# Values and normaliser of a head in one product over four banks, and the scores behind the second gate tile

## What is computed

```python
d = b[..., :, None] - b[..., None, :] + ic[..., None, :]          # decays, causal
m_t = jnp.maximum(m_inter, d.max(-1))
w_intra = jnp.exp(d - m_t[..., None]) * jnp.einsum('bhtd,bhsd->bhts', qc, kc)
w_inter = jnp.exp(m_inter - m_t)
num = w_inter[..., None] * jnp.einsum('bhtd,bhde->bhte', qc, C) + jnp.einsum('bhts,bhse->bhte', w_intra, vc)
nq = w_inter * jnp.einsum('bhtd,bhd->bht', qc, n) + w_intra.sum(-1)
h = num / jnp.maximum(jnp.abs(nq), jnp.exp(-m_t))[..., None]
C_new = decay[..., None, None] * C + jnp.einsum('bhs,bhsd,bhse->bhde', w_state, kc, vc)
n_new = decay[..., None] * n + jnp.einsum('bhs,bhsd->bhd', w_state, kc)
# then: hn = rmsnorm over the 256 values of a head; y = (hn * sigmoid(o)) @ w_out
```

## Time and profile before

| | us |
|---|---|
| runs of the kernel | 1204.06, 1206.19, 5891.28 (median 1206.19) |
| the profiled execution, its own time | 1204.14 |
| span of the profiled execution | 1202.3 |
| TensorE busy in the span | 1183.9 (98%) |
| VectorE, ScalarE, GpSimd busy | 861.8 (72%), 613.9 (51%), 175.6 (15%) |
| the part with the heads | about 122 to 225 of the span |

### The profile page before, as it was taken

One profiled execution on the slowest core, in us unless ns is written; L12 is line 12 of the kernel. 1 busy time (PEld: TensorE's weight loads), 2 busy tenths in 40 slices (PEclk: granted clock), 3 DMA queues, 4 the chain that ended last, 5 costly groups with the idle time before them and its releaser, 6 DMA issues.

```text
span 1202.3 us, 24151 instructions
## 1 busy us (share of the span) xinstructions
PE 1183.9 (98%) x9630; PEld 899.1 (75%) x9630; DVE 861.8 (72%) x1299; ACT 613.9 (51%) x1027; POOL 175.6 (15%) x285
## 2 busy tenths in 40 slices
PE   7999999999999999999999999999999999999998
PEld 6855777777777777777775456677777777787886
DVE  5744566587787888687774479758788878777664
ACT  6322354457555555454435459846555555554432
POOL 1000010001222233100003200000223222210001
PEclk9999999999999999999999999999999999999999
DMA  8643243234645645446646320022755455345662
GB/s 220 241 106 79 62 142 118 76 102 139 171 111 127 156 105 141 137 104 163 159 120 210 99 71 2 2 69 74 202 129 142 115 131 153 91 121 145 153 179 75
DMA packets 197195, 148.60 MB, mean 124 GB/s; under 512 B 5858, under 2 KB 178780, under 8 KB 196531
## 3 DMA queue, kind: packets, MB, share of 16 engines
q1 hardware_dynamic: 181562, 101.80, 29.5%
q0 software_dynamic: 15552, 45.68, 16.2%
HBM read 109.15 MB, written 9.86 MB: 99 GB/s over the span
## 4 chain that ended last, share of the span: by engine, by line
PE 86%; DVE 6%; ACT 4%; issue 2%; DMA 2%; POOL 0%; SPq 0%; DVEq 0%; POOLq 0%; ACTq 0%
PE PS L601 34%; PE PS L823 17%; PE PS L757 15%; PE PS L617 10%; DMA tL<-hidH 1%; PE PS L1632 1%; PE PS L1652 1%; DVE xT L649 1%; PE PS L1607 1%; DVE P L2659 1%; ACT ntmp L657 1%; DVE st L2640 1%; PE PS L1850 1%; PE PS L1883 1%; ACT wH L335 1%
## 5 line engine op out<-in xcount | busy, mean ns | idle before, releaser
L823 PE MATMUL PS<-hidH,blk 128*128 128x288 f16 x1232 | 227.9, 286 | 0.2 <-ACT val L546 0.2
L341 DVE SCALAR_TENSOR_TENSOR wL<-stage,wH 128x1024 f16<-128x1024 f32 x140 | 170.2, 1220 | 70.6 <-ACT wH L335 70.2
L335 ACT ACTIVATE wH<-stage 128x1024 f16<-128x1024 f32 x140 | 146.3, 1049 | 123.8 <-PE PS L617 56.6
L823 PE MATMUL PS<-hidL,blk 128*128 128x288 f16 x616 | 176.2, 286 | 0.0
L601 PE MATMUL PS<-zH,wH 128*128 128x288 f16 x832 | 170.1, 286 | 0.7 <-DVE zL L662 0.7
L601 PE MATMUL PS<-zL,wH 128*128 128x288 f16 x832 | 170.1, 286 | 0.0
L601 PE MATMUL PS<-zH,wL 128*128 128x288 f16 x832 | 170.1, 286 | 0.0
L823 PEld LDWEIGHTS PS<-hidH,blk 128*128 128x128 f16 x1232 | 120.5, 98 | 30.7 <-ACT val L546 0.6
L601 PEld LDWEIGHTS PS<-zH,wH 128*128 128x128 f16 x832 | 81.2, 98 | 22.0 <-DVE zL L662 1.3
L601 PEld LDWEIGHTS PS<-zL,wH 128*128 128x128 f16 x832 | 81.4, 98 | 20.5
L601 PEld LDWEIGHTS PS<-zH,wL 128*128 128x128 f16 x832 | 81.4, 98 | 20.5
(11 more groups left out here) (433 smaller groups left out, 2523.3 us busy)
## 6 DMA issues: line engine op xcount, KB each, us to landing
stage<-in_w_ffn_up SPq DMA_DIRECT2D x88, 512.0 KB, 4.2
quart<-in_w_ffn_down SPq DMA_DIRECT2D x32, 704.0 KB, 5.2
stage<-stage POOLq DMA_DIRECT2D x54, 256.0 KB, 4.8
stage<-in_w_mlstm_in SPq DMA_DIRECT2D x24, 512.0 KB, 5.0
stage<-in_w_swa_qkv SPq DMA_DIRECT2D x12, 512.0 KB, 4.6
quart<-quart POOLq DMA_DIRECT2D x8, 704.0 KB, 5.4
quart<-mixed POOLq DMA_DIRECT2D x8, 704.0 KB, 5.3
C<-in_state_mlstm_C POOLq DMA_DIRECT2D x4, 1024.0 KB, 7.7
```

The costliest lines, as they stand in the source:

```text
L335: nc.scalar.activation(wH[:, slot, :], stage[:, slot, :], ACT.Copy, scale=WSCALE).then_inc(hi_ready, inc)
L341: nc.vector.scalar_tensor_tensor(out=wL[:, slot, :], in0=stage[:, slot, :], scalar=WSCALE, in1=wH[:, slot, :], op0=ALU.mult, op1=ALU.subtr ...
L823: m = nc.tensor.matmul(down_bank(g), blk[:, g % RING, a, 128 * k:128 * (k + 1)], (hidH, hidL)[b][:, k, HIDDEN[j], :], start=(k == 0 and (a ...
```

## The change

For heads 0 to 2 each of the 4 chunks gets a bank of its own, in the order of `NUM_BANK`, (4, 5, 0, 2). A chunk's values and normaliser are then one product of 257 columns (`vM` with its column of ones, `Cst` with its last column), so the one-column matmuls are gone. Head 3 keeps the old form. As banks 0 and 2 now hold a part of the result until ScalarE has copied it, the decays and scores of the next head can't be written there before; `head_scores` is cut in two: `head_rows` (bank 1) stays where it was, and the rest, still called `head_scores`, comes behind the second gate tile for heads 1 to 3 and waits for `g`, the end of `head_gate(h-1)`. With it `head_exps` on ScalarE moves to behind `head_high(h-1)` and `head_weights` on VectorE to behind the second `gate_input`. The normaliser is read out of four banks by three copies instead of one, and ScalarE's first square waits for them instead of its fifth. Two waits for `w` are dropped.

```diff
@@ -1396,6 +1396,7 @@
         def turn_banks(h):
             return ((0, 2), 1) if h < MH - 1 else ((4, 5), 3)
 
+        NUM_BANK = (4, 5, 0, 2)
         MOUT_PAIR = (0, 3, 1, 2)
 
         QK_PAIR = (1, 0, 2, 1, 0, 2, 1, 3)
@@ -1575,18 +1576,22 @@
                                          start=(h == 0), stop=True, skip_group_check=True)
                 m.then_inc(hsem["nraw"], 1)
 
-            def head_scores(h):
+            def head_rows(h):
                 if h == 0:
                     pe.wait_ge(free["v"], TT + 8)
                     pe.wait_ge(gsem["parts"], 1)
                     pe.wait_ge(hsem["pad"], 1)
                 else:
-                    pe.wait_ge(hsem["w"], h)
                     pe.wait_ge(hsem["q"], h)
                 if h >= 2:
                     pe.wait_ge(hsem["g"], 2 * (h - 1))
                 sel = sel16[:, 128 * h:128 * (h + 1)]
                 nc.tensor.matmul(PS[:, 1, 0:RW], sel, R16[:, T:T + RW], start=True, stop=True).then_inc(hsem["r"], 1)
+
+            def head_scores(h):
+                if h:
+                    pe.wait_ge(hsem["g"], 2 * h)
+                sel = sel16[:, 128 * h:128 * (h + 1)]
                 nc.tensor.matmul(PS[:, 0, :], sel, R16[:, 0:SEQ], start=True, stop=False)
                 nc.tensor.matmul(PS[:, 0, :].rearrange("p (i t) -> p i t", i=4), ident16[:, :],
                                  cm16[:, :].unsqueeze(1).to_broadcast([128, 4, 128]), start=False,
@@ -1626,6 +1631,16 @@
                 hb = h % 2
                 pe.wait_ge(hsem["w"], h + 1)
                 pe.wait_ge(hsem["c"], 4 * h + 4)
+                if h < MH - 1:
+                    for i in range(4):
+                        out = PS[:, NUM_BANK[i], 0:DV + 1]
+                        m = nc.tensor.matmul(out, w4[:, hb, 128 * i:128 * (i + 1)], vM[:, i, h, :], start=True,
+                                             stop=(i == 0))
+                        if i:
+                            m = nc.tensor.matmul(out, qr[:, hb, 128 * (i - 1):128 * i], Cst[:, hb, i - 1, :],
+                                                 start=False, stop=True)
+                    m.then_inc(hsem["num"], 1)
+                    return
                 for i in range(4):
                     out, nq = PS[:, 4 + i // 2, DV * (i % 2):DV * (i % 2 + 1)], PS[:, 3, DV + 1 + i:DV + 2 + i]
                     w = w4[:, hb, 128 * i:128 * (i + 1)]
@@ -1656,7 +1671,6 @@
             def head_turn(h):
                 pe.wait_ge(hsem["f"], h + 1)
                 if h + 1 < MH:
-                    pe.wait_ge(hsem["w"], h + 2)
                     pe.wait_ge(hsem["q"], h + 2)
                 long, short = turn_banks(h)
                 for e in range(2):
@@ -1666,17 +1680,20 @@
                     m = nc.tensor.transpose(PS[:, short, 128 * e:128 * (e + 1)], ftok[:, 4, 128 * e:128 * (e + 1)], ident)
                 m.then_inc(hsem["t"], 1)
 
+            head_rows(0)
             head_scores(0)
             sample_weights()
             for h in range(MH):
                 if h:
-                    head_scores(h)
+                    head_rows(h)
                 gate_tile(2 * h)
                 head_states(h, (0, 1))
                 if h:
                     head_turn(h - 1)
                     head_states(h, (2, 3))
                 gate_tile(2 * h + 1)
+                if h:
+                    head_scores(h)
                 head_old_memories(h)
                 if h == 0:
                     head_states(h, (2, 3))
@@ -2054,14 +2071,18 @@
                     act.wait_ge(hsem["g"], 2 * h + e + 1)
                     nc.scalar.activation(gated(0, 2 * h + e), hs[:, e, :], ACT.Copy).then_inc(hsem["hi"], 1)
 
-            def num_of(tt):
-
-                return PS[:, 3, 0:DV] if tt == 4 else PS[:, 4 + tt // 2, DV * (tt % 2):DV * (tt % 2 + 1)]
+            def num_of(h, tt):
+
+                if tt == 4:
+                    return PS[:, 3, 0:DV]
+                if h < MH - 1:
+                    return PS[:, NUM_BANK[tt], 0:DV]
+                return PS[:, 4 + tt // 2, DV * (tt % 2):DV * (tt % 2 + 1)]
 
             act.wait_ge(gsem["m_out"], 32)
             for h in range(MH):
-                head_exps(h)
                 if h == 0:
+                    head_exps(h)
                     act.wait_ge(hsem["ss"], 1)
                     for g in range(MH):
                         m = nc.scalar.activation(ws64[:, g, :], PS[0:NS, 3, NS * g:NS * (g + 1)], ACT.Exp,
@@ -2070,21 +2091,22 @@
                 gate_sigmoid(2 * h)
                 if h:
                     head_high(h - 1)
+                    head_exps(h)
                 gate_sigmoid(2 * h + 1)
                 act.wait_ge(hsem["num"], h + 1)
                 if h:
                     act.wait_ge(hsem["z"], h)
                 for tt in range(TT):
-                    if tt == TT - 1:
+                    if tt == (TT - 1 if h == MH - 1 else 0):
                         act.wait_ge(hsem["nq"], h + 1)
-                    m = nc.scalar.activation(ftok[:, tt, :], num_of(tt), ACT.Square,
+                    m = nc.scalar.activation(ftok[:, tt, :], num_of(h, tt), ACT.Square,
                                              accum_out=stat[:, 0, (tt + 1) % TT:(tt + 1) % TT + 1])
                 m.then_inc(hsem["sq"], 1)
                 act.wait_ge(hsem["z"], h + 1)
                 link("A", act, nc.scalar.activation(stat[:, 2, :], stat[:, 2, :], ACT.Ln))
                 link("A", act, nc.scalar.activation(stat[:, 3, :], stat[:, 2, :], ACT.Exp, scale=-0.5))
                 for tt in range(TT):
-                    m = nc.scalar.activation(ftok[:, tt, :], num_of(tt), ACT.Copy,
+                    m = nc.scalar.activation(ftok[:, tt, :], num_of(h, tt), ACT.Copy,
                                              scale=stat[:, 3, (tt + 1) % TT:(tt + 1) % TT + 1])
                 m.then_inc(hsem["f"], 1)
             head_high(MH - 1)
@@ -2440,7 +2462,12 @@
                 dve.wait_ge(hsem["num"], h + 1)
                 if h:
                     dve.wait_ge(hsem["f"], h)
-                nc.vector.tensor_copy(stat[:, 1, :], PS[:, 3, DV:DV + TT]).then_inc(hsem["nq"], 1)
+                if h < MH - 1:
+                    nc.vector.tensor_copy(stat[:, 1, 0:3], PS[:, 3:6, DV])
+                    nc.vector.tensor_copy(stat[:, 1, 3:4], PS[:, NUM_BANK[2], DV:DV + 1])
+                    nc.vector.tensor_copy(stat[:, 1, 4:5], PS[:, NUM_BANK[3], DV:DV + 1]).then_inc(hsem["nq"], 1)
+                else:
+                    nc.vector.tensor_copy(stat[:, 1, :], PS[:, 3, DV:DV + TT]).then_inc(hsem["nq"], 1)
                 dve.wait_ge(hsem["nq"], h + 1)
                 link("V", dve, nc.vector.scalar_tensor_tensor(out=stat[:, 1, :], in0=stat[:, 1, :], scalar=EPS,
                                                               in1=stat[:, 1, :], op0=ALU.mult, op1=ALU.mult))
@@ -2499,8 +2526,7 @@
                 head_queries(h)
                 if h == 0:
                     sample_vectors()
-                head_weights(h)
-                if h == 0:
+                    head_weights(h)
                     sample_weights()
                 head_keys(h)
                 gate_input(2 * h)
```

## The result

| | before | after |
|---|---|---|
| median of 8 runs, us | 1203.86 | 1207.97 |
| range of ordinary runs, us | 1202.58 to 1206.19 | 1205.82 to 1209.70 |
| profiled execution, span, us | 1202.3 | 1204.7 |
| TensorE busy in the span, us | 1183.9 | 1182.9 |
| first gate tile of head 0 to the start of `mout`, us | 99.2 | 102.2 |

The ratio of after to before is 1.0031, 95% interval 1.0022 to 1.0041: slower by 3.7 us (the medians differ by 4.1), and clear of noise. Level within a microsecond was forecast, and the range ended at 1207.3. In one run of the kernel before, 5891.28 us is an outlier and counts for nothing.

A forecast was written before the change was run, and what follows sets the result against it. TensorE, busy 98% of the span, was taken as the bound, with gate tiles between heads timed by VectorE. Values savings of -1.53 us and scores costs of +1.40 summed to -0.4: 1204.14 to 1203.7 us, range 1200.8 to 1207.3.

The forecast's parts named there:

- Values stage: TensorE, heads 0 to 2: seven products of 257 columns take 3.15 us instead of 4.68, saving 1.53 us per head.
- Scores in the open: Behind the second gate tile, heads 1 to 3: decays and scores cost 1.40 us each, including 0.07 for a break.
- The gate tile timed by the updates: Between heads, VectorE's memory updates release the gate tile, 2.97 us after the values stage, untouched by the change.
- The stall: TensorE's idle time between heads, ahead of the gate tile, grows from 0.22 to 1.7 us.
- Slack of the normaliser: VectorE ahead of the memory updates: 0.33 us left, at worst 0.09, so the added copies cost nothing.
- rival B: VectorE, L2443 to L2468: normaliser copies and split use up the slack, updates start late; 1204.9 us, chance 0.18.
- C: The scores' results come late and the values wait for `w`, 1.8 us of cover gone; 1206.7 us, chance 0.03.
- A: The whole saving arrives, with updates ready as soon as TensorE is; 5.3 us in all, 1198.9 us, chance 0.06.
- The sum: At the end of head 3: -1.79 + 1.40 = -0.4 us, giving 1203.7 us; bounds -0.9 and +1.4.
- The range: Whole kernel: 1200.8 to 1207.3 us, from its own 1203.2 to 1205.5 and 2.1 us between ordinary runs.
- rival D: Stalls between heads drop TensorE's clock; three gate tiles at 1.2 GHz, 18 us more, 1222 us, chance 0.02.

The follow-up runs named there:

- the second profile: The profile of the changed kernel timed once more with no edit; 1206.60 us, ratio 1.0026 to the kernel before.
- three extra products: Changed kernel with three unread float32 products of 64 columns ahead of the rows product of heads 1 to 3; median 1204.26 us, ratio 1.0007 to before.
- The kernel with six products: Changed kernel with six unread float32 products of 64 columns ahead of the rows product of heads 1 to 3; 1202.86 us against 1203.56 before.

## Why the prediction was wrong

The sum for work and waits was right, and a rival that the prediction gave 2 in 100, the clock, came on top of it.

- **Values stage**: forecast 3.15 us, measured 3.23 (168.09 to 171.32), at 0.43 for the products behind the first. Saved 1.45 instead of 1.53 us a head.
- **Scores in the open**: forecast 1.40 us, measured 1.33 (163.83 to 165.16). The 0.07 us for a break at their wait stood in no row, and nothing of it was measured.
- **The gate tile timed by the updates**: right. From the end of the values stage to the gate tile it is 174.29 - 171.32 = 2.97 us, the very number of before. Forecast starts 1.5 and 1.7 us earlier in heads 1 and 2; measured 148.92 and 174.29 against 150.41 and 175.90, 1.49 and 1.61. In head 3 it was 1.8 forecast and 0.06 measured (201.34 against 201.40), since the fall in head 2 took 1.67 of it; and `mout` starts 2.95 us later (228.00 against 225.05) instead of 0.4 earlier. The stall is 1.55 us, forecast 1.7: the rows product keeps TensorE busy for 0.36 us, and the forecast took the 0.20 to the start of the next product.
- **Slack of the normaliser** (rival B): three copies and the updates still wait. VectorE in order of time, 163 to 178 us:

```profile
171.43 0.16 DVE L2466 COPY stat<-PS 128x3 f32<-128x3 f32 x1
...
171.57 0.15 DVE L2468 COPY stat<-PS 128x1 f32<-128x1 f32 x1
...
172.58 1.66 DVE L2495 SCALAR_TENSOR_TENSOR C<-C,dec,PS 128x256 f32<-128x256 f32 x4 [0.46 <-PE PS L1667]
```

  0.46 us of slack, forecast 0.33; B did not happen. The values never wait for `w` (C), and A is out, as the update chain decides.
- **The sum**: forecast -0.4 us. The heads' part gives +3.00 with 3.34 of falls, so -0.34; in the second profile +2.79 - 3.17 = -0.38; with three extra products -0.35. That it came out so near was in part luck: per head the saving was 0.08 us too high and the price of the scores 0.07 too high, and the two cancel (3 x (1.33 - 1.45) = -0.36). The kernel with six products measures -0.7 us by its times, by an interval that reaches from -1.7 to +0.5.
- **The range**: a slip in its upper end. 1205.5 and 2.1 are 1207.6, not 1207.3; the measured 1207.97 lies outside either.
- **The clock** (rival D) is the step that failed, in its chance and in its price. It rested on the earlier trace rows: the idle time at the start of the program with the clock at 1.00. TensorE in order of time, 0 to 8 us, shows where in these 10 us it stands idle in the kernel before:

```profile
5.92 0.99 PE L1416 MATMUL PS<-C,rowsD 5*128 5x5 f32 x8 [5.92 <-DMA rowsD<-in_mlstm_head_norm]
```

  That is idle time ahead of the first work, not between two pieces of it, and no evidence on a stall in the middle. And "no stall of this size in a busy stretch of this trace shows a fall" was said of a trace whose longest stall between two pieces of work is the 1.18 us above, and 0.22 among the heads: none of 1.7 was there to show a fall or its absence. The price, a whole tile at 1.2 GHz in each of three heads, was 18 us; a fall lasted about 3 to 3.5 us and cost 1.4 to 1.7, so that three of them are 5 us. Priced like that, the rival would have given 1205.4 to 1208.7 us, and it would have been worth holding in the range.

The Trainium skill, TensorE: Matmul & The Clock Gate, section "HAM oscillation — how this bites in real kernels", tells of bursts of matmuls parted by waits for DMA, each of which starts again at the slow clock and pays for it anew. The trace agrees in kind, with a gate tile of 7.72 us instead of 6.05 behind a stall. The waits in the page's own case are about 3 to 5 us, so by the page alone a stall of 1.55 us was not to be feared; here the measurement decides.

What stays open is why, of three equal stalls, only one or two brought a fall in the profiles, and another one in another kernel. Only two of the changed kernel's 18 runs have a profile, both with two falls and a granted clock of 0.997. In the first eight runs those at 0.997 took 1205.82 to 1207.45 us and those at 0.995 or 0.996 took 1208.48 to 1209.70, so the slower ones probably had three falls or more; a run at 0.999 took 1204.01 us, with one fall or none. How many each run had, and where, isn't shown.

## What to carry to other kernels

Work that TensorE does while it would otherwise wait for another engine can do more than fill time: here it kept TensorE's clock at full speed. Before moving such work away, look at the idle time that stays behind, and price it twice, as a stall and as a possible 1.4 to 1.7 us more for the matmuls behind it. A clock that the trace before shows at 1.00 says nothing of a stall that this trace doesn't have. The granted clock of each run, beside its time, tells whether falls came in runs that have no profile. If the move is needed, shorten the chain that the stall waits for (here: the sample product ahead of the last values, the updates ahead of the normaliser), so that both halves of the gain arrive.

## What was not expected of the hardware

- A stall of 1.55 us between busy stretches was enough for the granted clock to go to 1.2 GHz for about 3 to 3.5 us, though not each time (7 of 12 such stalls in the four profiles with it; the changed kernel two of three, twice). A wait of 1.44 us for a DMA at the start of another kernel brought one too. With 0.84 us the one profile has none, but the granted clock of the runs shows falls in at least four of eleven. With 0.22 and 0.50 us none was seen in the profiles.
- A stall of 1.18 us in another part of the program brought none in twelve profiles of twelve, so the length alone doesn't decide.
- A float32 product of 64 columns behind another takes 0.23 us (ten in 2.28), where one of 257 takes 0.43: a quarter of the columns isn't a quarter of the time.
- One-column float32 products cost 1.46 us in a head for 7 of them, 0.21 each, part of it as slower products behind them (0.54 against 0.43).
